# Experts' gate and up weights: two transfers of half the features each in place of one

## The reference, cut to what matters

```
hid = silu(einsum('nd,edf->nef', xf, w_gate)) * einsum('nd,edf->nef', xf, w_up)
out = einsum('nef,ne,efd->nd', hid, combine, w_down)
```

## Time and profile before

| | |
|---|---|
| runs | 2148.97 us median, 2146.13 to 2151.54 |
| profiled execution: its own time, its span | 2145.22 us, 2143.1 us |
| TensorE's granted clock, mean | 0.911 |
| TensorE (PE) busy | 1848.7 us (86%) |
| VectorE (DVE), ScalarE (ACT), GpSimd (POOL) busy | 759.5, 350.2, 66.1 us |
| products with gate and up weights, L2036 | 244.0 us busy; idle before them 32.6 us, 30.9 us of it ended by these weights' DMA |
| products with down weights, L2060 | 116.9 us busy, 2.5 us idle |
| gate and up loads, L1929 | 64 of 2048 KB |
| down loads, L1933 | 64 of 1024 KB |
| SP's DMA queue | 408.63 MB of the 441.05 MB moved |
| DMA rate in the slices of the experts' stages | 315 to 423 GB/s; mean over the span 206 |

### The profile page before, as it was taken

One profiled execution on the slowest core, in us unless ns is written; L12 is line 12 of the kernel. 1 busy time (PEld: TensorE's weight loads), 2 busy tenths in 40 slices (PEclk: granted clock), 3 DMA queues, 4 the chain that ended last, 5 costly groups with the idle time before them and its releaser, 6 DMA issues. The chain is left out here.

```text
span 2143.1 us, 22565 instructions
## 1 busy us (share of the span) xinstructions
PE 1848.7 (86%) x8114; PEld 1088.9 (51%) x8114; DVE 759.5 (35%) x1560; ACT 350.2 (16%) x524; POOL 66.1 (3%) x68
## 2 busy tenths in 40 slices
PE   4999999889889959988479999997998898599883
PEld 2666657456446634433236666674574475343231
DVE  2243357563223342211324234475631242332113
ACT  1013212141101021110001312122311201211000
POOL 0000000000000001111000000000000000011110
PEclk8999999896999979999779999997979999699996
DMA  7565422323364179999366652223235631999982
GB/s 291 184 228 187 138 93 79 118 72 108 119 216 167 69 315 373 422 423 421 120 267 215 220 176 98 102 79 130 68 109 167 216 122 58 370 418 423 423 350 75
DMA packets 107127, 441.05 MB, mean 206 GB/s; under 512 B 19394, under 2 KB 54498, under 8 KB 79746
## 3 DMA queue, kind: packets, MB, share of 16 engines
q1 hardware_dynamic: 79442, 408.63, 50.4%
q10 hardware_dynamic: 18352, 20.40, 3.0%
q0 software_dynamic: 9216, 10.51, 1.4%
HBM read 433.70 MB, written 28.84 MB: 216 GB/s over the span
## 5 line engine op out<-in xcount | busy, mean ns | idle before, releaser
L367 PE MATMUL ps<-s_proj_and_h,w_in_tiles 128*128 128x320 f32 x1280 | 354.4, 438 | 8.3 <-PEq L203 8.3
L367 PEld LDWEIGHTS ps<-s_proj_and_h,w_in_tiles 128*128 128x128 f32 x1280 | 243.9, 192 | 123.4 <-issue 26.7
L177 PE MATMUL ps<-s_proj_and_h,w_in_tiles 128*128 128x320 f32 x960 | 290.8, 452 | 1.2 <-ACT s_proj_and_h L187 1.2
L2036 PE MATMUL ps<-s_proj_and_h,t_ex_xf 128*64 128x512 f32 x1024 | 244.0, 632 | 32.6 <-DMA s_proj_and_h<-w_gate_up 30.9
L177 PEld LDWEIGHTS ps<-s_proj_and_h,w_in_tiles 128*128 128x128 f32 x960 | 185.0, 198 | 88.4 <-issue 25.8
L2036 PEld LDWEIGHTS ps<-s_proj_and_h,t_ex_xf 128*64 128x64 f32 x1024 | 82.9, 146 | 189.9 <-issue 189.9
L1742 PE MATMUL ps<-s_proj_and_h,w_merge 128*128 128x320 f32 x512 | 138.3, 433 | 3.8 <-PEq L1664 3.8
L1742 PEld LDWEIGHTS ps<-s_proj_and_h,w_merge 128*128 128x128 f32 x512 | 97.1, 190 | 45.1 <-issue 4.9
L2060 PE MATMUL ps<-w_down_slots,t_ex_hf 128*64 128x512 f32 x512 | 116.9, 598 | 2.5 <-DVE t_ex_hf L2107 1.0
L2105 DVE TENSOR_TENSOR t_ex_hid<-t_ex_hid,ps 128x256 f32<-128x256 f32 x32 | 13.5, 421 | 254.4 <-ACT t_ex_hid L2131 254.4
L1972 POOL DMA_INDIRECT rt_h_tm<-h_rows,t_ex_token x32 | 33.9, 1060 | 1635.0 <-DMA h_rows<-rt_h_tm 810.8
(11 more groups left out here) (424 smaller groups left out, 2012.4 us busy)
## 6 DMA issues: line engine op xcount, KB each, us to landing
s_proj_and_h<-w_gate_up SPq DMA_DIRECT2D x64, 2048.0 KB, 29.9
w_in_tiles<-w_in SPq DMA_DIRECT2D x140, 512.0 KB, 3.6
w_down_slots<-w_down SPq DMA_DIRECT2D x64, 1024.0 KB, 30.9
w_mod_panels<-w_mod SPq DMA_DIRECT2D x32, 1024.0 KB, 7.3
page_keys<-pages_k SPq DMA_DIRECT2D x128, 192.0 KB, 3.3
s_proj_and_h<-w_mod SPq DMA_DIRECT2D x16, 1024.0 KB, 12.3
w_merge<-w_branch SPq DMA_DIRECT2D x16, 1024.0 KB, 4.9
page_values<-pages_v ACTq DMA_DIRECT2D x96, 128.0 KB, 2.8
```

Of the source, the lines that this page charges most:

```text
L177: mm = pe.matmul(K.ps[:, self.BANKS[i % 2], 0:T], self.win[:, j, k, :], K.h[:, k, :], start=(k == 0), stop=(k == KD - 1))
L367: mm = pe.matmul(K.ps[:, n % BANKS, 0:T], win[:, j, k, :], K.h[:, k, :], start=(k == 0), stop=(k == KD - 1))
L2036: mm = pe.matmul(K.ps[rows, GU, :], xf[:, k, rows], K.gate_up[:, j, k, :], start=(k == 0), stop=(k == KD - 1))
```

## The change

`load_expert` issues two loads for an expert: the first four steps of 128 features (the lower half) with the semaphore `gu_low_loaded`, then the other four with `gu_high_loaded`. Each is 1 MB, in runs of 8 KB per partition. TensorE waits for the lower halves of both experts of the pair ahead of the first step, and for the upper halves of both ahead of the fifth. The loads of a pair thus stand in the queue as low and high of the first expert, low and high of the second. Nothing else changes.

```
@@ load_expert
-    s = K.sem
-    sp.dma_start(K.gate_up[:, j], K.d["w_gate_up"][l, e].rearrange("o p k n -> p (o k) n")).then_inc(s(f"gu_loaded{j}"), 16)
+    s, src = K.sem, K.d["w_gate_up"][l, e].rearrange("o p k n -> p (o k) n")
+    sp.dma_start(K.gate_up[:, j, 0:KD // 2], src[:, 0:KD // 2]).then_inc(s(f"gu_low_loaded{j}"), 16)
+    sp.dma_start(K.gate_up[:, j, KD // 2:KD], src[:, KD // 2:KD]).then_inc(s(f"gu_high_loaded{j}"), 16)
@@ experts_stage, the program of TensorE
                 for _, _, j, count in experts(p):
-                    pe.wait_ge(s(f"gu_loaded{j}"), count)
+                    pe.wait_ge(s(f"gu_low_loaded{j}"), count)
                 if p:
                     pe.wait_ge(s("hid_ready"), p)
                 for k in range(KD):
+                    if k == KD // 2:
+                        for _, _, j, count in experts(p):
+                            pe.wait_ge(s(f"gu_high_loaded{j}"), count)
                     for q, rows, j, _ in experts(p):
                         mm = pe.matmul(K.ps[rows, GU, :], xf[:, k, rows], K.gate_up[:, j, k, :],
```

## The result

The changed kernel takes 2162.83 us (median of 7 runs, 2157.7 to 2170.0), the kernel before, run beside it, 2146.13 us (7 runs, 2144.69 to 2151.54). The ratio is 1.0074, with a 95% interval of 1.0053 to 1.0096. That is 16.7 us slower, where 13.3 was forecast, and the time is in the forecast's range. The profiled execution has a span of 2155.6 us, 12.5 more than before.

The account below looks back on a forecast made before the run. Bound by the experts' weight stream at full DMA rate plus a 6 us hole set by pair 0's start. Barrier 10.0 + 9.7, gathers -4, ends -2.4 give +13.3 us: 2148.97 to 2162 us, range 2152 to 2176.

Parts of the forecast that it names:

- Where the loss is: At the norm's barrier (L281) before the router: SP's held load issues delay everything behind it; 9.7 to 11.2 us a layer.
- Barrier: Norm's barrier L281: SP arrives at 781.4 us instead of 771.4; 10.0 us lost in the first layer, 9.7 in the second.
- Loads, or their rows: SP's DMA queue: at most ten loads outstanding; the limit counts loads or their 128 rows each, not bytes.
- Gathers: Token gather before pair 0: issued later, it meets less traffic and gives back some 2 us a layer, bounds 0 and 3.
- The halves' cost in the stream: Refill stream behind the hole: 0.05 us a load over 26 loads, 1.3 us a layer, bounds 0 to 2.6.
- The gain at the end: Last pair's gate and up products: start 2.5 us ahead of the last landing, net 1.2 us sooner a layer.
- The absolute time: Whole kernel: 2162 us, from a median of 2148.97 us for the kernel before plus 13.3.
- The change does not do what it says: Rival at the last pair: halves land together, nothing starts sooner, the end costs 1.3 us a layer; 2167 us, 8%.
- The page's rule of 341 GB/s for 1 MB transfers: Weights' stream: 6.15 us for 2 MB instead of 4.93, 64 us for both layers, 2226 us; rival at 2%.

Follow-up runs that it names:

- e3: The changed kernel, all loads still halves, with seven of the 18 issues moved behind the norm's barrier; 2144.97 us, ratio 0.9989 to the kernel before.
- e6: The kernel before, whole gate and up loads, plus five small 128-row loads, so 18 loads stand ahead of the barrier; 2160.98 us, ratio 1.0083.
- e2: The kernel before, first filling's gate and up loads split by partitions into two of 64: 18 loads, no more rows; 2214.31 us, ratio 1.0303.
- e8: The kernel before plus five small loads of 16 rows (128 in e6), again 18 loads ahead of the barrier; 2161.9 us, ratio 1.0064.
- e9: Like e3, but refills come in quarters of 0.5 MB with 4 KB rows, each released and waited for by itself; 2149.03 us, ratio 1.0012.
- e1: The changed kernel with the first filling in whole loads (13 ahead of the barrier), only refills in halves; 2153.83 us, ratio 1.0017 to the kernel before.

## Why the prediction was right, point by point

- **Where the loss is: right, and shown.** Taking the 18 loads away from the barrier with all halves kept (e3) removes the loss; adding the delay with no halves (e6) makes it, ratio 1.0083 against the change's 1.0074.
- **Barrier, 10.0 + 9.7 us forecast.** SP went from 0.1 us behind DVE to 10.8 and from 0.4 us ahead of it to 10.3 behind; as DVE set the second barrier before, that is 10.6 and 10.3 us, 1.2 more in all than forecast. Pair 0 was nevertheless 7.6 + 8.0 = 15.6 us late, against 15.7 forecast, because the stretch from the barrier to the gather was 0.4 and 0.9 us shorter than before (26.6 us from SP's drain to the gather in the first layer, 27.0 before). That these two cancel is luck. The end of the last issue was forecast as the landing of the eighth load plus 0.3; it was that plus 1.1 (778.3 against 777.2).
- **"Loads, or their rows."** The prediction left this open, and for this change it made no difference, as every load has 128 rows. e2 and e8 show that neither alone is right: rows and one entry more per load fit all four kernels.
- **Gathers, 4 us back forecast: 2.7 + 1.3 = 4.0 us.** Right in sum, not for each.
- **The halves' cost in the stream, 1.3 us a layer: too small.** From the first refill's issue to the last landing it was 213.6 and 215.3 us before and 215.9 and 217.7 after, 2.3 us a layer; to the last gate and up landing, which the sum needs, 1.7 us longer in both layers. Both are inside the bound of 2.6.
- **The gain at the end, net 1.2 us a layer: its first part came, the net did not.** The last products began 2.2 us ahead of the last gate and up landing instead of 0.3 behind it, the 2.5 us that the prediction names. From pair 0's start to the end of the last down product the stages still took 0.7 and 0.1 us longer than before. The stream took 1.7 us of the 2.5 in each layer. In the first layer the last pair waited 2.84 us and its products took 8.78 us instead of 7.08, the loss that the prediction had in its bounds and not in its sum. In the second layer the products of pair 0 took 9.42 us instead of 8.59, which it did not foresee. This is the term that was mis-sized: 2.4 us of gain forecast, 0.8 us of loss measured, 3 us in both layers, and the reason why 16.3 us were measured in the stages and 13.3 forecast.
- **The absolute time, 2162 us forecast and 2162.83 measured: so close by luck.** The forecast stood on 2148.97 us for the kernel before, which ran at 2146.13 beside the changed one. The difference, 16.7 against 13.3 us, is the fair comparison.
- **"The change does not do what it says"** was a rival at 8%, 2167 us. Its price of 1.3 us at the end of each layer is nearer to what was measured than my own term. But the halves did land apart, 2.5 us each, and the products did start on the third of the pair's four, so its mechanism is not what happened.
- **The page's rule of 341 GB/s for 1 MB transfers**, from the Trainium skill's page "DMA: Bandwidth & Descriptors", section Bandwidth: with all loads of 1 MB the stream ran at 419 GB/s. The trace does not agree with it for queued loads. The prediction's 6.15 us for 2 MB is worked out from the rate; the page's table has 6.15 us as the time of the 1 MB transfer itself, while queued loads of 1 MB landed 2.5 us apart here. The rule's direction shows in e9: with gate and up loads of 0.5 MB in 4 KB rows the stream ran at 407.

## What to carry to other kernels

Ahead of a barrier, an engine that only issues loads is not free: once its queue is full, each issue waits for a landing, and the barrier waits with it. Before a load is split, count how many loads and rows stand between the engine and its next barrier, and move what doesn't fit behind it. Where a stream runs at full rate, earlier arrival at the consumer is worth nothing until the stream ends (here 2.5 us at the last pair, eaten by slower refills); what a split can give is the earlier release of the slot, and only while the stream has a hole to fill.

## What was not expected of the hardware

- Loads into 64 of the 128 partitions kept all 16 DMA engines busy at about half their rate. Their packets of 16 KB took 1228 ns in the mean in e2's first filling, against 618 in the kernel before. The 8 KB packets of the down loads between them, into all partitions, took 469 ns instead of 310. Together that is 238 GB/s with a share of 1.01, against 420 GB/s.
- A small delay at the barrier can cost more than itself. In e8 the router's products began 4.0 us later behind the first issue than before, and pair 0 began 6.8 us later (54.96 against 48.12 us). Of the 2.8 us added on the way, 1.1 are the router's products, 7.44 us for 6.30, and 1.8 the gather, 10.1 us for 8.3:

```profile
770.40 7.44 PE L1829 MATMUL ps<-s_proj_and_h,w_router_ 128*36 128x320 f32 x16 [15.01 <-PEq L281]
...
770.40:777.84 7.44, 7.44 (x17) 2.60 (x18) 0.09 (x1) 0.00 (x0) 0.00 (x0) 0.60 1.00 423
```

  The granted clock over these products was 0.60, nearer to the lower level of 1.2 GHz, and 0.71 before. In the second layer of e1, 1.9 us became 5.4, with the same two parts: 7.40 us at 0.60 for the products, 10.1 us for the gather. A delay of 10.6 us, on the other hand, cost 7.6: the products took 6.16 us at 0.72, after an idle time of 21.63 us, and the gather ran as the first filling ended. Why the clock was lower after the idle times of 15.0 and 12.7 us than after 11.0 and 21.6, and why the gather is slowest when issued a few us late, was not tried and stays open.
- The kernel before is near this edge itself: SP and DVE met at the barrier within 0.4 us. The spread of e1's runs (2142.8 to 2160.3 us), with SP 1.9 us late in the one layer seen, fits that. It was not shown that this is what spreads them.
